# A two-layer attention, convolution and feed-forward trunk on one core: the first modulation rows in four column strips, the gate's sigmoid behind the exponentials, branch chunks split one query tile later, and odd query tiles of layer two with the first map's low parts between the two maxima

## What is computed

```python
mod = jax.nn.silu(c) @ w_mod[l] + b_mod[l]            # and the same for c_ctx
h  = modulate(rms_norm(x, g_norm1[l]), sh1, sc1)      # h * (1 + scale) + shift
gq, gk, gv, dq, dk, dv, cu = project_heads(h @ w_in[l], ...)
o_gqa  = softmax attention, 8 query heads on 2 key heads
w = p[:, :, 0] - lam * p[:, :, 1]                     # differential attention: two maps
u = a * jax.nn.sigmoid(g)                             # a, g: halves of cu, then width-31 convolution
y = g_a * y_a + g_b * y_b + g_c * y_c                 # three branches, gated; then @ w_out
x = x + gt1 * y;  x = x + gt2 * swiglu(modulate(rms_norm(x, g_norm2[l]), sh2, sc2))
```

## Time and profile before

| what | value |
|---|---|
| three runs | 2377.58, 2379.27, 2379.94 us; median 2379.27 |
| the profiled execution | 2377.62 us, span 2375.8 us |
| busy | PE 97%, PE weight loads 87%, DVE 57%, ACT 43%, POOL 36% of the span |
| granted TensorE clock, mean | 0.995 of full |
| moved by DMA | 208.96 MB, 88 GB/s over the span |

### The profile page before, as it was taken

How to read it: one execution, slowest core, us unless ns; L and a number is a source line. 1 busy time by engine, 2 the same in 40 slices (tenths; PEclk the granted TensorE clock), 3 DMA queues, 4 the chain that set the end, 5 groups by cost and what they waited for, 6 DMA issues and landing times.

```text
span 2375.8 us, 32833 instructions
## 1 busy us (share of the span) xinstructions
PE 2302.5 (97%) x12832; PEld 2073.7 (87%) x12832; DVE 1359.5 (57%) x2068; ACT 1018.6 (43%) x1991; POOL 854.8 (36%) x593
## 2 busy tenths in 40 slices
PE   7999999999999989999999999999999999999999
PEld 4888899999999989999999997778878877888887
DVE  5566677699976745654443347667889845111111
ACT  4666676652252342212212237667654254322222
POOL 2566312100034424453333335752220243544443
PEclk9999999999999999999999999999999999999999
DMA  6101111123224523434343431111103323333333
GB/s 260 46 19 36 37 36 36 32 85 94 67 71 138 173 70 112 137 108 133 116 141 97 126 98 54 32 41 45 54 27 103 106 94 106 104 98 95 98 94 97
DMA packets 134665, 208.96 MB, mean 88 GB/s; under 512 B 12528, under 2 KB 66032, under 8 KB 134384
## 3 DMA queue, kind: packets, MB, share of 16 engines
q1 hardware_dynamic: 134512, 206.86, 27.5%
HBM read 202.62 MB, written 4.19 MB: 87 GB/s over the span
## 4 chain that ended last, share of the span: by engine, by line
PE 80%; DVE 11%; ACT 3%; issue 2%; DMA 1%; SPq 1%; POOL 1%; DVEq 0%; ACTq 0%
PE acc L717 21%; PE acc L719 21%; PE acc L718 21%; DVE X L1841 4%; PE sco L916 3%; PE aux L717 3%; PE aux L719 3%; PE aux L718 3%; PE aux L929 2%; PE acc L951 2%; DVE NM L1753 1%; DVE RB L1707 1%; PE aux L894 1%; DVE M L1707 1%; DVE WLO L1707 1%
## 5 line engine op out<-in xcount | busy, mean ns | idle before, releaser
L610 POOL TENSOR_TENSOR WLO<-STG,WHI 128x512 fp32r<-128x512 f32 (+2 forms) x500 | 691.8, 1404 | 1407.3 <-ACT WHI L1177 1242.3
L717 PE MATMUL acc<-H,WHI 128*128 128x384 f32 (+2 forms) x1976 | 711.6, 360 | 16.9 <-DVE H L2006 8.3
L719 PE MATMUL acc<-H,WLO 128*128 128x384 f32 (+2 forms) x1976 | 694.5, 351 | 0.0
L718 PE MATMUL acc<-H,WHI 128*128 128x384 f32 (+2 forms) x1976 | 693.9, 351 | 0.0
L1177 ACT ACTIVATE WHI<-STG 128x512 fp32r<-128x512 f32 (+2 forms) x616 | 331.0, 586 | 395.6 <-PE acc L719 354.0
L717 PEld LDWEIGHTS acc<-H,WHI 128*128 128x128 f32 x1976 | 373.2, 189 | 46.3 <-issue 16.7
L719 PEld LDWEIGHTS acc<-H,WLO 128*128 128x128 f32 x1976 | 372.8, 189 | 25.5
L718 PEld LDWEIGHTS acc<-H,WHI 128*128 128x128 f32 x1976 | 373.6, 189 | 24.1 <-issue 0.2
L717 PE MATMUL acc<-RB,WHI 128*128 128x384 f32 (+1 forms) x816 | 288.6, 354 | 3.2 <-DVE RB L1707 1.4
L719 PE MATMUL acc<-RB,WLO 128*128 128x384 f32 (+1 forms) x816 | 287.6, 352 | 0.0
L718 PE MATMUL acc<-RB,WHI 128*128 128x384 f32 (+1 forms) x816 | 287.5, 352 | 0.0
(11 more groups left out here) (160 smaller groups left out, 2830.1 us busy)
## 6 DMA issues: line engine op xcount, KB each, us to landing
STG<-in_w_fi SPq DMA_DIRECT2D x176, 256.0 KB, 2.7
M<-in_w_mod SPq DMA_DIRECT2D x56, 512.0 KB, 4.6
STG<-in_w_in SPq DMA_DIRECT2D x104, 256.0 KB, 2.6
STG<-in_w_gate SPq DMA_DIRECT2D x96, 256.0 KB, 2.7
STG<-in_w_fo SPq DMA_DIRECT2D x64, 256.0 KB, 2.7
STG<-in_w_br SPq DMA_DIRECT2D x96, 128.0 KB, 2.1
FIRST<-in_w_mod SPq DMA_DIRECT2D x8, 1024.0 KB, 20.2
SOONB<-in_w_mod SPq DMA_DIRECT2D x16, 512.0 KB, 4.2
```

The source lines that it names most:

```text
L610: nc.gpsimd.tensor_tensor(WLO[:, s, a:a + w], STG[:, g, a:a + w], WHI[:, s, a:a + w].bitcast(F32), ALU.subtract).then_inc(S("w_split"), 1)
L717: nc.tensor.matmul(dst, lh, rh, start=first, stop=False)
L718: nc.tensor.matmul(dst, lh, rl, start=False, stop=False)
L719: return nc.tensor.matmul(dst, ll, rh, start=False, stop=last)
```

## The change

It has four parts.

- **Opening.** Each `first_rows` matmul now has 32 columns of weights (`SCW`: two of SiLU(c), thirty zeros) and writes its own 32 of PSUM's 128 partitions, strip k mod 4, so chunks k and k+4 share a strip. `first_row` copies 128 partitions, and `first_turn` is a matmul with `FROW` as weights and a 128x2 selector `SEL`, which sums the four strips as it turns them. `FIRST` moves in SBUF, so that groups 2 to 7 no longer lie under H. SP's order becomes x in two halves, groups 0 and 1, the two weight tiles of the pair, groups 2 to 7. The angles' table and `WDW` now wait until all eight rows are computed (`SCW` lies in the table's place), and the weight tiles behind them on SP wait with them. PE has only groups 0 to 3 ahead of the pair; groups 4 to 7 stand between its chunks (`ahead`). ACT's and DVE's orders in the first norm follow.
- **The gate's sigmoid** and its two table loads move from the last slot of a tile to the next head's tile 0, behind its exponentials; `gate_conv` moves behind that tile's maxima and probabilities. Four places in each layer.
- **branch_lo** of chunks 0, 1, 2 moves from the end of tiles 0, 1, 2 of head 7 to the middle of tiles 1, 2, 3.
- **Odd tiles of layer two**: `turned_lo` of the first map stands between the two maxima, not behind both.

```diff
-        FROW = [G[0:2, 16 + 256 * i:16 + 256 * (i + 1)] for i in range(2)]
+        FROW = [G[:, 256 * i:256 * (i + 1)] for i in range(2)]
+        SCW = v4(K, K_COS, KC, 32)
+        SEL = RLN[:, 0:2]
...
+            for i in range(2):
+                sp.dma_start(X[:, 4 * i:4 * i + 4, :], xT[:, 4 * i:4 * i + 4, :]).then_inc(S(f"x{i}"), 16)
             first_groups(0)
-            sp.dma_start(X[:, :, :], xT).then_inc(S("x"), 16)
+            tile(w_in[0, 0], KC * P)
+            tile(w_in[0, 2], KC * P)
             for i in range(1, MOD_FIRST // 2):
                 first_groups(i)
...
-                    if l == 0 and t == 2:
+                    if l == 0 and t == 1:
+
+                        sp.wait_ge(S("f_full"), MOD_FIRST)
                         sp.dma_start(K[:, 0:K_ONES], consts[:, 0:K_ONES]).then_inc(S("angles"), 16)
...
                 for k in range(KC):
-                    mm = nc.tensor.matmul(sco[0][0:2, 512 * (n % 2):512 * (n % 2) + MOD_GROUP], SC[:, k, :],
+
+                    q = slice(32 * (k % 4), 32 * (k % 4) + 32)
+                    mm = nc.tensor.matmul(sco[0][q, 512 * (n % 2):512 * (n % 2) + MOD_GROUP], SCW[:, k, :],
                                           FIRST[:, 2 * n + k // 4, k % 4 * MOD_GROUP:(k % 4 + 1) * MOD_GROUP],
-                                          start=k == 0, stop=k == KC - 1)
+                                          start=k < 4, stop=k >= 4)
...
+                              ahead={0: [(first_rows, 4)], 1: [(first_rows, 5), (first_turn, 4)], 2: [(first_turn, 5), (first_rows, 6)],
+                                     3: [(first_rows, 7), (first_turn, 6), (first_turn, 7)]} if l == 0 else {})
...
                             if done:
-                                act.wait_ge(S(f"acc_free{banks['acc'][u][0]}"), banks["acc"][u][1] + 2)
-                                fn(XG[:, 1, 0:n], XG[:, 1, 0:n], ACT.Sigmoid, sem="sig")
-                                exp_set()
+                                staged.append((l, banks["acc"][u]))
...
+                    if j >= 4 and i == 0:
+                        gate_sigmoid()
...
                     if after:
                         maximum(0, g + 1, after[3])
+                    if l and i % 2:
+                        turned_lo((l, g, 0), PTS[0], P * (i % 2), k0)
                     if after:
                         maximum(1, g + 1, after[3])
-                    turned_lo((l, g, 0), PTS[0], P * (i % 2), k0)
+                    if l == 0 or i % 2 == 0:
+                        turned_lo((l, g, 0), PTS[0], P * (i % 2), k0)
...
+                    if j == HEADS - 1 and 0 < i < 4:
+                        branch_lo(l, i - 1)
```

More of the change, by code:

```diff
@@ L542, in _ @@
             for l in range(DEPTH):
-                for t in [0, 2, 1, 3, *range(4, 10)]:
+                for t in [0, 2, 1, 3, *range(4, 10)][2 if l == 0 else 0:]:
                     tile(w_in[l, t], KC * P)
@@ L639, in _ @@
             nc.gpsimd.memset(WDW[:, :, :, TAPS:4 * TAPS4], 0.0).then_inc(S("wdw_zero"), 1)
+            nc.gpsimd.memset(SCW, 0.0).then_inc(S("scw_zero"), 1)
             nc.gpsimd.memset(SCX[:, :].bitcast(F32), 0.0).then_inc(S("scx_zero"), 1)
@@ L748, in tile, with tile_pair @@
                 c.step("tile")
-            def tile_pair(rngs, others, ready, name, other, sem="h_ready", lag=0):
+            def tile_pair(rngs, others, ready, name, other, sem="h_ready", lag=0, ahead={}):
                 t = c.at("tile")
@@ L756, in tile_pair @@
                 for step in range(KC + lag):
+                    for run, group in ahead.get(step, ()):
+                        run(group)
                     for n, k in enumerate((step, step - lag)):
@@ L1297, in attention, with gate_sigmoid @@
                 n = n_tok(l)
+                staged = []
+                def gate_sigmoid():
+                    bank, before = staged.pop()[1]
+                    act.wait_ge(S(f"acc_free{bank}"), before + 2)
+                    fn(XG[:, 1, 0:n], XG[:, 1, 0:n], ACT.Sigmoid, sem="sig")
+                    exp_set()
                 def slot(j, s, later=False):
@@ L1524, in _ @@
             act.wait_ge(S("silu_c"), 1)
+            act.wait_ge(S("scw_zero"), 1)
+            fn(SCW[:, :, 0:2], SC[:, :, :], ACT.Copy, sem="scw")
             act.wait_ge(S("scx_zero"), 1)
@@ L1535, in first_row @@
                     act.wait_ge(S("f_turned"), n - 1)
[L1536 removed]
+                fn(FROW[n % 2], sco[0][:, 512 * (n % 2):512 * (n % 2) + MOD_GROUP], ACT.Copy, sem="f_row")
+            for j in range(KC):
+                if j % 4 == 0:
+                    act.wait_ge(S(f"x{j // 4}"), 16)
+                fn(MM[:, j, :], X[:, j, :], ACT.Square, sem="nsq")
             first_row(0)
             first_row(1)
[L1540 to L1544 removed]
+            hi()
             for l in range(DEPTH):
@@ L1868, in slot @@
                         values_lo((l, j, "vt"), kv_buffer(j))
-                    if j >= 4 and s == last["g"]:
-                        gate_conv(l, j - 4)
                 maximum(0, 0, 0)
@@ L2084, in _ @@
             dve.wait_ge(S("consts"), 16)
+            nc.vector.tensor_reduce(SEL, IDENT.rearrange("p (t c) -> p c t", c=32)[:, 0:2, :], AX_X, ALU.add).then_inc(S("sel"), 1)
             dve.wait_ge(S("lams"), 16)
@@ L2110, in _ @@
                 own("nadd", tt(T[:, :], T[:, :], MM[:, i, :], ALU.add))
-            for i in range(2):
-                first_sum(2 * i)
-                first_sum(2 * i + 1)
-                first_gain(i)
+            first_sum(0)
+            first_sum(1)
+            first_gain(0)
             for l in range(DEPTH):
```

52 lines of the change are left out of this document (26 added, 26 removed).

## The result

| | before | changed |
|---|---|---|
| median of 4 runs each | 2378.43 us | 2363.49 us (2361.66 to 2367.76) |
| ratio, 95% interval | | 0.9939 (0.9922 to 0.9957) |
| profiled execution, span | 2377.62, 2375.8 us | 2363.59, 2361.8 us |

A forecast was written before the change was run, and what follows sets the result against it. PE was taken as the bound, at nine tenths or more in all slices but the first; -10.1 - 4.3 - 1.2 - 1.9 = -17.5 on 2377.62 gave 2360.1, stated as 2361 for the median, range 2353 to 2370.

The forecast's parts named there:

- Term one, the opening, -10.1: Before layer one's values tile: strips and the new order start that tile at 56.8 instead of 66.86, -10.1 us.
- a group's 1.75 us: PE's rows in the opening: a group on four strips takes 1.75 us, half of the 3.5 before.
- the bound from below: PE's rows in the opening: a group could cost a quarter, 0.9 us, with the values tile at 53.4 (-13.5).
- lower bound for serial strips, -2.4: Opening, rival: strips run one after another, 3.5 us a group, values tile about 64.5, -2.4; time 2367.8, chance 0.13.
- Branch_lo and sigmoid in layer two's head 7, -4.3: Layer two's head 7: PE waits of 1.43, 1.91, 0.64 and 0.86 go, 0.5 comes back in tile 1: -4.3 us.
- Layer one, -1.2: Layer one's attention: PE waits of 0.42 and 0.54 go, and 0.2 at head 4: -1.2 us.
- the 0.2 forecast at head 4: Layer one's head 4: the evacuation that PE waits 2.68 us for becomes free about 0.2 us earlier.
- Odd tiles, -1.9: Layer two's odd tiles: 0.9 won in tile 3 of three heads (2.7), 0.8 lost in tile 1: -1.9 us.
- The differential heads have several us, so nothing: Odd tiles of the differential heads: several us lie between probabilities and their use, so the edit changes nothing there.
- attention's waits only move: Attention, rival: old waits are replaced by others a tile later, terms two and three are nought: 2367.5, chance 0.12.
- The attention's terms, forecast at 7.4: Attention of both layers: -4.3 in layer two's head 7, -1.2 in layer one, -1.9 in odd tiles.
- The moved loads: Angles, `WDW` and fourth weight tile wait for the last rows: hidden by the pair, 5 us to spare, no cost.

The follow-up runs named there:

- opening only: The changed kernel with its three attention edits undone (sigmoid and its multiplication, branch_lo, odd tiles as before): median 2368.50 us, ratio 0.9955 to the kernel before.

## Why the prediction was right, and where not

- **Term one, the opening, -10.1: right, -11.2** in the profile, -12.9 where the clock didn't fall. Landings came as worked out from the mean flow (15.05, 17.73, 20.20, 28.03, 30.78 against 15.1, 17.6, 20.2, 27.9, 30.5), R ended at 26.2. The term in it that was mis-sized is a group's 1.75 us: the next operation starts 1.0 behind three of the four groups and 1.8 behind group 4, 4.8 in all for 7.0, so the bound from below was the nearer one. The turns between the chunks took 1.9, where 1.0 was put down, and the pair with its share of the lower clock 18.1, where 18.3 was. The Trainium skill's factor for column strips ("TensorE: Matmul & The Clock Gate", Part 3), 2.38 times for three, would have been the better guide: in proportion 1.1, an estimate. The Trainium skill's rule (same page and part, "The mechanism") that a weight load passes matmuls only if its row group differs did not hold these strips apart: of group 5, four matmul records start within 0.02 us of each other and the next four 0.24 us later, where in one place one record follows the other after 0.22, and the weight loads of the next four stand beside the first four.
- **What the term rests on.** The forecast split it into strips and order; the runs show that neither gives anything alone (values tile 67.96 and 68.44, medians 2379.39 and 2378.61, the latter even with the attention's edits), both together 11. The strips take PE's work away, the order takes R, ACT's rows and DVE's sums away from in front of it. The forecast's lower bound for serial strips, -2.4 with the values tile at 64.5, was wrong too: it went from group 4's landing, and PE would still be at group 2 then (68.44 measured).
- **Branch_lo and sigmoid in layer two's head 7, -4.3: the step failed.** "Three convolution taps still stand ahead of the maximum and now hold it back by about 0.5": it was 2.65, and 1.0 at the lower clock behind it. 4.84 of waits went, 3.65 came: -1.2. In the forecast's terms, the path of the sigmoid's two table loads was missing. I had followed ACT's queue behind the sigmoid to the keys and the `aux` bank only, and had written that "in head 7 nothing is put in the place of what leaves". The sub norm's factor was: the sigmoid's own two table loads hold it 1.54. And the three taps took 4.29 us, while POOL made low parts from 1738.35 to 1741.35, where they take 2.32 with the sigmoid at its old place. With the taps moved head 7 gives 5.4 against the kernel before.
- **Layer one, -1.2: right in size.** Against opening only the changed kernel gains 1.3 from 411 to 475. The waits of 0.42 and 0.54 are gone; the 0.2 forecast at head 4 didn't come (2.67 after 2.68), and 0.3 came from the sigmoid instead. Another 0.9 behind it, a wait for `WLO` that was 1.37 before, is 0.38, 1.06, 0.80 and nothing in other profiles, after openings that differ: it goes with the phase, and I count it to no edit.
- **Odd tiles, -1.9: the step failed, and the term is nought** (+0.9 in the grouped heads, -0.8 in head 7). Per grouped head the edit won 0.69 in tile 3, not 0.9, and cost 0.26 at the scores, which I hadn't seen, and 0.65 to 0.74 in tile 1, not 0.2: 0.3 lost in each of three heads. "The differential heads have several us, so nothing" was wrong as well: 0.8 won in head 7. The rival "attention's waits only move" described these two terms better than the forecast did.
- **The sum, right with some luck.** -11.2 for the opening, -1.3 and -0.9 in layer one, +0.9 in the grouped heads and -1.2 in head 7 (its 0.8 of the odd tiles is in it) make -13.7; the span has -14.0 (the forecast's own sum on the median comes to 2361.8, for which it gave 2361). The 0.3 between them is within the clock: the profile of the kernel before has six falls to the lower level, of 3.4 or 6.8 us each, the changed kernel's two have six and eight, most of them at the same places of the program, and where one profile has a fall and another hasn't, its lead moves by 1.0 to 1.7 us. The attention's terms, forecast at 7.4, gave 1.6, or 2.5 with the wait for `WLO`. The sum came within 3.5 us all the same, because the opening gave 1.1 more than forecast and layer one 0.9 that no term has, and because the range took in the rival with these terms at nought (2367.5); 2363.49 lies between it and the forecast.
- **What cost nothing.** The moved loads, `SEL` and the keys' evacuation, as forecast: from 33 to 82 us PE has one wait over 0.2, of 0.58, and it had one of 0.59 there before.

## What to carry to other kernels

Work taken off the engine that bounds a stretch pays only when what stands in order behind it on the other engines is moved too; test each half alone before you credit either. When an instruction is moved back in a queue, follow everything that it now holds up at its new place, in each tile of the head, and count what shares the engine's time there. And make an edit where its wait is: the same reordering won 0.7 us a head in tile 3 and lost 0.7 in tile 1, and 0.3 more at the scores.

## Unexpected on the hardware

- Column strips overlap nearly whole: 3.61, 1.92 and 1.07 us for one group in one, two and four places, 1.9 and 3.4 times.
- The same wait of PE is followed by a fall of the granted clock in one execution and not in another: 0.56 and 1.00 behind 2.41 us, in two kernels, and behind 2.39 us in two executions of the changed kernel.
- PE's first groups took 1.94 us, the pace of a recorded 0.50, ahead of the first clock that the trace lists (24.1 us); the 1.00 of a window there is an empty list.
- DVE's taps of 128x512 take longer when they start beside POOL's subtractions. Of the three in a row, the first ended as POOL began and took 0.74; the next two took 1.80 and 1.67 (the shortest, middle and longest of the view, in ns):

```profile
L1871 DVE SCALAR_TENSOR_TENSOR X<-U,WDW,X x3: 743/1667/1804, 1737.6 to 1740.2; 128x512 f32<-128x512 f32 x3
1738.35 3.00 POOL L618 TENSOR_TENSOR WLO<-STG,WHI 128x512 fp32r<-128x512 f32 x2 [5.74 <-ACT WHI L1194]
```

In this trace none of the 107 taps of this size that ran without such a subtraction took over 0.76. With the sigmoid at its old place POOL begins during the third, and the same three take 2.32 together, 0.75 each. No run moved POOL's work alone.
